# Retention scores from a head's parts stacked on 128 partitions

## The reference, cut to what matters

```
def _retention(q, k, v, gn_gain):
    q = _rope(q, pos, dk, RET_ROPE_THETA) * (dk ** -0.5)
    k = _rope(k, pos, dk, RET_ROPE_THETA)
    log_g = jnp.log(1.0 - 2.0 ** (-5.0 - jnp.arange(H, dtype=jnp.float32)))
    ...
    decay = jnp.where(diff >= 0, jnp.exp(jnp.maximum(diff, 0.0) * log_g[:, None, None]), 0.0)
    ...
    inner = jnp.einsum('bhncd,bhnkd->bhnck', qc, kc) * decay[None, :, None].astype(dt)
    o_inner = jnp.einsum('bhnck,bhnke->bhnce', inner, vc)
    ...
    mu = jnp.mean(o, axis=-1, keepdims=True)
    var = jnp.mean(jnp.square(o - mu), axis=-1, keepdims=True)
    on = (o - mu) * lax.rsqrt(var + GN_EPS) * gn_gain.astype(jnp.float32)[None, :, None, :]
```

## Time and profile before

| what | value |
|---|---|
| median of 3 runs | 2146.44 us (2146.4 to 2148.82) |
| the profiled execution's own time | 2147.04 us |
| span of its trace | 2145.2 us |
| its mean granted TensorE clock | 0.993 |
| PE busy | 98% of the span |
| DVE, ACT, POOL busy | 62%, 47%, 33% |

### The profile page before, as it was taken

One profiled execution on the slowest core, in us unless ns is written; L12 is line 12 of the kernel. 1 busy time (PEld: TensorE's weight loads), 2 busy tenths in 40 slices (PEclk: granted clock), 3 DMA queues, 4 the chain that ended last, 5 costly groups with the idle time before them and its releaser, 6 DMA issues.

```text
span 2145.2 us, 31345 instructions
## 1 busy us (share of the span) xinstructions
PE 2110.5 (98%) x10842; PEld 1784.4 (83%) x10842; DVE 1324.4 (62%) x2182; ACT 1007.1 (47%) x1771; POOL 701.9 (33%) x523
## 2 busy tenths in 40 slices
PE   8999999999999999999999999999999999999998
PEld 6878888888888888898887788888877888888886
DVE  5467774466762276775268788788768336676523
ACT  4345664543442253444234567777646325334322
POOL 2011345323233261443327701211155415133331
PEclk9999999999999999999999999999999999999998
DMA  5211235334433333443234322222264533434321
GB/s 171 79 47 67 84 112 190 101 122 153 150 124 108 98 108 113 161 138 123 94 101 156 118 69 75 79 75 79 94 202 138 185 99 118 135 132 167 104 93 65
DMA packets 73423, 248.15 MB, mean 116 GB/s; under 512 B 8080, under 2 KB 8336, under 8 KB 72944
## 3 DMA queue, kind: packets, MB, share of 16 engines
q1 hardware_dynamic: 51120, 182.08, 26.0%
q0 software_dynamic: 10496, 37.56, 5.1%
q10 hardware_dynamic: 11712, 27.27, 3.5%
HBM read 227.48 MB, written 18.87 MB: 115 GB/s over the span
## 4 chain that ended last, share of the span: by engine, by line
PE 83%; DVE 8%; ACT 2%; POOL 2%; issue 2%; DMA 1%; DVEq 0%; POOLq 0%; SPq 0%; ACTq 0%
PE bank L188 24%; PE bank L190 24%; PE bank L189 24%; PE bank L194 3%; PE bank L195 3%; POOL hid L738 2%; PE bank L2128 2%; DVE w_lo L162 1%; DMA w_raw<-stream 1%; DVE gn_r L2730 1%; PE bank L912 1%; DVE xn_lo L608 1%; ACT w_hi L157 1%; DVE h L622 1%; POOL hid L1471 1%
## 5 line engine op out<-in xcount | busy, mean ns | idle before, releaser
L162 DVE TENSOR_TENSOR w_lo<-w_raw,w_hi 128x1024 fp32r<-128x1024 f32 x337 | 454.8, 1353 | 425.1 <-ACT w_hi L157 422.2
L188 PE MATMUL bank<-xn_hi,w_hi 128*128 128x512 f32 (+1 forms) x1432 | 554.7, 387 | 4.1 <-DVE w_lo L162 2.6
L157 ACT ACTIVATE w_hi<-w_raw 128x1024 fp32r<-128x1024 f32 x337 | 354.7, 1054 | 414.0 <-PE bank L190 248.2
L189 PE MATMUL bank<-xn_lo,w_hi 128*128 128x512 f32 (+1 forms) x1432 | 539.1, 376 | 0.0
L190 PE MATMUL bank<-xn_hi,w_lo 128*128 128x512 f32 (+1 forms) x1432 | 538.8, 376 | 0.0
L188 PEld LDWEIGHTS bank<-xn_hi,w_hi 128*128 128x128 f32 x1432 | 271.1, 189 | 56.6 <-DVE h L622 5.2
L190 PEld LDWEIGHTS bank<-xn_hi,w_lo 128*128 128x128 f32 x1432 | 269.8, 188 | 50.2
L189 PEld LDWEIGHTS bank<-xn_lo,w_hi 128*128 128x128 f32 x1432 | 271.0, 189 | 45.7 <-issue 2.9
L188 PE MATMUL bank<-down_hi,w_hi 128*128 128x512 f32 x528 | 205.8, 390 | 0.0
L190 PE MATMUL bank<-down_hi,w_lo 128*128 128x512 f32 x528 | 205.4, 389 | 0.0
L189 PE MATMUL bank<-down_lo,w_hi 128*128 128x512 f32 x528 | 205.4, 389 | 0.0
(11 more groups left out here) (462 smaller groups left out, 4272.7 us busy)
## 6 DMA issues: line engine op xcount, KB each, us to landing
w_raw<-stream SPq DMA_DIRECT2D x337, 512.0 KB, 3.5
s_raw<-stream POOLq DMA_DIRECT2D x48, 512.0 KB, 6.3
spill_g<-gate_out ACTq DMA_DIRECT2D x16, 256.0 KB, 2.0
m_more<-spill_g POOLq DMA_DIRECT2D x3, 1024.0 KB, 12.5
x<-xt SPq DMA_DIRECT2D x4, 512.0 KB, 7.1
x<-xt ACTq DMA_DIRECT2D x1, 2048.0 KB, 9.3
spill_x<-x ACTq DMA_DIRECT2D x1, 2048.0 KB, 6.5
spill_ga<-ga_out ACTq DMA_DIRECT2D x8, 256.0 KB, 2.1
```

Of the source, the lines that this page charges most:

```text
L157: nc.scalar.activation(w_hi[:, slot, :], w_raw[:, slot % 2, :], ACT.Copy).then_inc(split_hi, 1)
L162: nc.vector.tensor_tensor(w_lo[:, slot, :], w_raw[:, slot % 2, :], w_hi[:, slot, :], ALU.subtract).then_inc(split_lo, 1)
L188: nc.tensor.matmul(to, a_hi, b_hi, start=start, stop=False, skip_group_check=True)
L189: nc.tensor.matmul(to, a_hi, b_lo, start=False, stop=False, skip_group_check=True)
```

## The change

`stage` and `stage_low` take the place of `high_qk` and `low_qk`, and are called for each of the eight heads. Of head h, with its rows r and the other 64 rows: ACT writes the high query to `rq_both[r]`, the high key to `rk_own[h % 2][r]` and again to `rk_mixed[other]`; POOL subtracts the low query into `rq_rest[r]`, a new tile, copies it with a DMA of its queue to `rq_both[other]` (128 KB within the on-chip memory), and subtracts the low key into `rk_mixed[r]`. The other rows of the two `rk_own` tiles are set to zero once. So `rk_own` times `rq_both` is hi*hi, and `rk_mixed` times `rq_both` is lo*hi + hi*lo: `score` issues two matmuls over 128 rows for each block in place of three over 64, eight for a head in place of twelve. It waits for the three high parts, the two low parts and the copy. `rq_both` and `rk_mixed` are single buffers, so the staging of a head waits for the scores of the head before.

Head 0 is staged within sparse attention, head 1 before iteration 0 (on ACT after the first loads of values and before highs(0), on POOL before lows(0)), and head h+2 in iteration h. In iteration 0, score(1) moves behind the second half of the fill.

```diff
--- before.py
+++ after.py
@@ -1700,6 +1700,8 @@
         rq_lo = sb("rq_lo", [P, S], F32R, A0 + 50 * K)
         rk_hi = sb("rk_hi", [P, S], F32R, A0 + 52 * K)
         rk_lo = sb("rk_lo", [P, S], F32R, A0 + 54 * K)
+        rq_both, rk_mixed, rk_own = rq_hi, rk_lo, (rk_hi, rq_lo)
+        rq_rest = sb("rq_rest", [P, S], F32R, A0 + 14 * K)
         decay = sb("decay", [P, 2, S], F32, A0 + 56 * K)
         rv_hi = sb("rv_hi", [P, 2, 2, S], F32R, A0 + 80 * K)
         rv_lo = sb("rv_lo", [P, 2, 2, S], F32R, A0 + 88 * K)
@@ -2551,6 +2553,7 @@
                                               "out", "square", "var", "root", "recip", "done", "gated", "cleared")}
             decay_in, rv_in = ([sem(f"ret_{n}_in{k}") for k in range(2)] for n in ("decay", "rv"))
             gr_in, r_low = sem("ret_gr_in"), sem("b2_r_low")
+            crossed, c_at, zeroed, z_at = sem("ret_crossed"), 0, att_sems["mask"], 3
             y = merge_sems
             y0 = merges["y"]
             fgm, fm = FIRST["b2_gm"], FIRST["b2_merge"]
@@ -2563,16 +2566,27 @@
             def score_bank(kb):
                 return (banks[0][:], banks[1][:, 0:384], banks[2][:, 0:256], banks[1][:, 384:S])[kb]
 
-            def high_qk(act, pair):
-                at_least(act, s["scored"], 8 * pair)
-                act.wait_ge(nsa["r_done"], 5 + pair)
-                nc.scalar.activation(rq_hi[:], r_qk[:, pair, :], ACT.Copy).then_inc(s["staged_hi"], 1)
-                nc.scalar.activation(rk_hi[:], r_qk[:, 4 + pair, :], ACT.Copy).then_inc(s["staged_hi"], 1)
-
-            def low_qk(pool, pair):
-                for n, (to, hi) in enumerate(((rq_lo, rq_hi), (rk_lo, rk_hi))):
-                    pool.wait_ge(s["staged_hi"], 2 * pair + n + 1)
-                    nc.gpsimd.tensor_tensor(to[:], r_qk[:, 4 * n + pair, :], hi[:], ALU.subtract).then_inc(s["staged_lo"], 1)
+            def stage(act, h):
+                at_least(act, s["scored"], 4 * h)
+                act.wait_ge(nsa["r_done"], 5 + h // 2)
+                r, other = halves(h % 2)
+                q, k = r_qk[r, h // 2, :], r_qk[r, 4 + h // 2, :]
+                nc.scalar.activation(rq_both[r, :], q, ACT.Copy).then_inc(s["staged_hi"], 1)
+                nc.scalar.activation(rk_own[h % 2][r, :], k, ACT.Copy).then_inc(s["staged_hi"], 1)
+                nc.scalar.activation(rk_mixed[other, :], k, ACT.Copy).then_inc(s["staged_hi"], 1)
+
+            def stage_low(pool, h):
+                r, other = halves(h % 2)
+                pool.wait_ge(s["staged_hi"], 3 * h + 1)
+                at_least(pool, crossed, 16 * h, c_at)
+                nc.gpsimd.tensor_tensor(rq_rest[r, :], r_qk[r, h // 2, :], rq_both[r, :], ALU.subtract
+                                        ).then_inc(s["staged_lo"], 1)
+                pool.wait_ge(s["staged_lo"], 2 * h + 1)
+                pool.dma_start(rq_both[other, :], rq_rest[r, :]).then_inc(crossed, 16)
+                pool.wait_ge(s["staged_hi"], 3 * h + 2)
+                nc.gpsimd.tensor_tensor(rk_mixed[r, :], r_qk[r, 4 + h // 2, :], rk_own[h % 2][r, :], ALU.subtract
+                                        ).then_inc(s["staged_lo"], 1)
+                pool.wait_ge(s["staged_lo"], 2 * h + 2)
 
             def decay_to(pool, h):
                 if h < 2:
@@ -2583,20 +2597,28 @@
                 pool.dma_start(decay[:, h % 2, :], decays[h]).then_inc(decay_in[h % 2], 16)
 
             def first_act(act):
-                high_qk(act, 0)
+                act.wait_ge(zeroed, z_at + 2)
+                stage(act, 0)
 
             def first_pool(pool):
-                low_qk(pool, 0)
+                for tile in rk_own:
+                    nc.gpsimd.memset(tile[:].bitcast(F32), 0.0).then_inc(zeroed, 1)
+                pool.wait_ge(zeroed, z_at + 2)
+                stage_low(pool, 0)
                 decay_to(pool, 0)
                 decay_to(pool, 1)
 
             def score(pe, h):
-                r = slice(64 * (h % 2), 64 * (h % 2) + 64)
-                pe.wait_ge(s["staged_lo"], 2 * (h // 2 + 1))
+                pe.wait_ge(s["staged_hi"], 3 * (h + 1))
+                pe.wait_ge(s["staged_lo"], 2 * (h + 1))
+                pe.wait_ge(crossed, 16 * (h + 1) + c_at)
                 for n, kb in enumerate(ORDER_K):
                     at_least(pe, s["weighted"], 4 * (h - 1) + (1, 3, 3, 4)[n])
-                    mm3(score_bank(kb), rk_hi[r, kb * P:(kb + 1) * P], rk_lo[r, kb * P:(kb + 1) * P],
-                        rq_hi[r, kb * P:S], rq_lo[r, kb * P:S]).then_inc(s["scored"], 1)
+                    w, to = slice(kb * P, (kb + 1) * P), score_bank(kb)
+                    nc.tensor.matmul(to, rk_own[h % 2][:, w], rq_both[:, kb * P:S], start=True, stop=False,
+                                     skip_group_check=True)
+                    nc.tensor.matmul(to, rk_mixed[:, w], rq_both[:, kb * P:S], start=False, stop=True,
+                                     skip_group_check=True).then_inc(s["scored"], 1)
 
             def first_pe(pe):
                 score(pe, 0)
@@ -2635,10 +2657,9 @@
                     fill(h, slot, range(0, 4))
                     if h:
                         values(h)
-                    else:
-                        score(pe, 1)
                     fill(h, slot, range(4, KT)).then_inc(used, 1)
                     if h == 0:
+                        score(pe, 1)
                         pe.wait_ge(nsa["out"], 16 + nsa_outs)
                         values(0)
                 squares_summed(HEADS - 1)
@@ -2672,6 +2693,7 @@
 
                 act.wait_ge(rv_saved, 32 * HEADS)
                 values_in(0)
+                stage(act, 1)
                 highs(0)
                 act.wait_ge(gr_saved, 16 * HEADS)
                 act.wait_ge(ga_saved, 16 * HEADS)
@@ -2681,8 +2703,8 @@
                         values_in(1)
                     elif h % 2 == 0 and h < 6:
                         values_in(h // 2 + 1)
-                    if h % 2 == 0 and h < 6:
-                        high_qk(act, h // 2 + 1)
+                    if h + 2 < HEADS:
+                        stage(act, h + 2)
                     if h + 1 < HEADS:
                         highs(h + 1)
                     ahead(high_part, act, fgm, h)
@@ -2693,7 +2715,7 @@
                     at_least(act, s["var"], h)
                     nc.scalar.activation(gn_sq[:], banks[6 + h % 2][:], ACT.Square).then_inc(s["square"], 1)
                     for k in A_TILES.get(h, ()):
-                        act.wait_ge(s["staged_lo"], 8)
+                        act.wait_ge(s["staged_lo"], 16)
                         act.wait_ge(nsa["out"], 16 + nsa_outs)
                         nc.scalar.activation(a_hi[:, k, :], a_raw[:, k, :], ACT.Copy).then_inc(y["y_hi"], 1)
                     if h == HEADS - 1:
@@ -2761,10 +2783,13 @@
                         nc.gpsimd.tensor_tensor(ws_lo[:, KOFF[kb]:KOFF[kb + 1]], weighted[:, KOFF[kb]:KOFF[kb + 1]],
                                                 ws_hi[:, KOFF[kb]:KOFF[kb + 1]], ALU.subtract).then_inc(s["lo"], 1)
 
+                pool.wait_ge(nsa["r_done"], KT)
+                stage_low(pool, 1)
                 lows(0)
                 for h in range(HEADS):
-                    if h % 2 == 0 and h < 6:
-                        low_qk(pool, h // 2 + 1)
+                    if h + 2 < HEADS:
+                        pool.wait_ge(s["lo"], 4 * (h + 1))
+                        stage_low(pool, h + 2)
                     if h + 2 < HEADS:
                         decay_to(pool, h + 2)
                     if h + 1 < HEADS:
```

## The result

The changed kernel takes 2157.54 us (median of 8 runs, 2153.43 to 2159.34); runs of the kernel before beside it give 2146.95 (8 runs, 2144.89 to 2150.14). The ratio is 1.0047, with a 95% interval of 1.0036 to 1.0058: 10.1 us slower, 7.7 to 12.5. I had forecast 2151.1 and a range up to 2157. The sign is right, the loss is twice mine.

The account below looks back on a forecast made before the run. PE's instructions and a ring of the other engines were both taken to need about 10.6 us a head; start +2.1, low clock +1.65 and collisions +0.9 made +4.7 us, forecast 2151.1 us, range 2143 to 2157.

Parts of the forecast that it names:

- the two waits for copies: At retention's start PE waits 2.8 us for score(1) and about 5 us for score(2), until the staging copies land.
- the ring: Later heads: the closed chain weigh, ws_hi, w_hi, w_lo, reciprocal, two products, weigh, without PE's matmuls, takes 10.6 us a head.
- the ring's collisions: Later heads: POOL's subtractions in the new stagings of iterations 3 and 5 lengthen DVE's L2738; +0.9 us, bounds 0 and 2.9.
- the low clock: Behind PE's waits at the start, matmuls run at the lower clock again; +1.65 us, bounds 0 and 1.65.
- the landing time L: Time from issue to landing of each of the first two staging copies; 4.5 us, between 2.5 and 6.2.
- Ring and PE: Later heads: PE would take 9.6 us against 10.6 for the other engines' chain, and wait for gn_sq by the difference.
- What PE saves: Each head's score drops the third product and takes about 1.3 us; 0.93 us saved a head, 7.4 in all.
- Place and form of the start's loss: Heads 1 and 2 are staged serially, each after the scores before; values(1) come 2.1 us later, bounds -1.9 and +5.5.
- my own steps: Start: first copy issued at 1561.1, second at 1564.5 + L, values(1) at 1569.5 + 2L, L being the copy's landing time.
- The ceiling of 2.6 us: Later heads: by the Trainium skill, each new staging could cost a whole subtraction, 2.6 us for the two iterations.
- Hidden parts: ACT's three instructions and later heads' copies cost nothing; a copy may land 4.3 us after issue without a wait.
- the heavy start: Rival: copies take 6.2 us at the start and collisions occur in every iteration; +10.1 us, 2156.5 us; chance 0.16.

Follow-up runs that it names:

- experiments 1: The kernel before with score in two 128-row matmuls per block, own staging kept, both cross products left out; 0.9994 of before.
- 7: The kernel before with ACT issuing w_hi ahead of the high parts of the next head's scores; 0.9999 of before.
- 8: The kernel before with two 128-row matmuls per block (not the reference's scores) and w_hi ahead of the next head's high parts; 0.9971 of before.
- Experiment 5: The changed kernel with a second rq_both and rk_mixed, heads 1 and 2 staged earlier, rq_rest still single; 1.0046 of before.
- Experiment 3: The changed kernel with gr_silu and the values of head pair 1 (3 MB) issued after w_hi of iteration 0; 1.0060 of before.
- experiment 13: The changed kernel with 16 and 27 filler matmuls into an unused bank ahead of score(1) and score(2); 1.0042 of before.
- experiment 2: The changed kernel with ACT copying the low query to the other 64 rows in place of POOL's DMA; 1.0027 of before.
- experiment 9: The changed kernel with two buffers by the head's parity and ACT's copy of the low query in place of the DMA; 1.0024 of before.

## Why the prediction was right and where it failed

What failed are terms of the sum: the two waits for copies, their places and the ring as the pace of the later heads are as forecast, but the +4.7 us are 9.2 in retention. Too small were the ring's collisions (+0.9, measured +2.2), the low clock (+1.65, measured 2.7), the landing time L (4.5 us, measured 5.1 and 4.9, with 0.27 and 0.19 from there to the matmul), and POOL's wait for its own semaphore before the second issue (nothing, measured 0.3). L failed in kind too, as is shown below.

**Ring and PE: right.** That the 0.93 us a head would not count is shown by experiments 1, 7 and 8 together. One refinement: with its ring relieved the kernel before keeps iterations of 10.56 us (7). PE is its bound, the ring stands right behind; the order in which I had them mattered for nothing.

**What PE saves: right.** A burst of 1.26 us, as worked out. Later iterations take 9.51 to 9.64 us wherever the ring lets them.

**Place and form of the start's loss: right; its size wrong.** Taking off the 1.94 us that came up earlier, the first copy is issued at 1561.23 (forecast 1561.1). From there, by my own steps:

- score(1) starts 5.37 us after the issue, where I had L = 4.5: 5.1 to the landing and 0.27 from there to the matmul, with the forecast issue 0.1 too early as well: +1.0 us.
- From score(1) to the second issue 4.04 us for 3.4; 0.3 of it is POOL's wait for its own subtraction, which no step of mine had: +0.64.
- Second copy 4.9 us, 0.19 more to the matmul: +0.59.
- score(2) to values(1) 7.69 us for 5.0 + 1.65: +1.04, the low clock.

These make 3.3 us, the difference of 7.06 and the forecast 2.1 + 1.65.

**The term that failed in kind is L.** I took the landing for a duration behind the issue, mid-way between rows of a loaded and an unloaded queue. Experiment 5 shows that it isn't: issued 1.9 us earlier, the copy lands at the same place. Experiment 3 shows what it hangs on: without the 3 MB the second copy takes 2.2 us, and where they go the delay goes. In six profiles the first copy lands 0.3 to 0.7 us behind rv_lo, the last load issued before it. That is no rule either. In experiment 13 rv_lo lands at 18.85, but gr_silu is issued only 0.14 us behind the copy (1.26 us in the changed kernel), and the copy lands at 22.28, after 7.4 us; in experiment 5 the second copy lands at 27.87, 2.1 us before the last of the loads issued ahead of it. Which loads a copy waits behind stays open. The numbers 5.1 and 4.9 fell inside my bounds, so as a size L was off by 0.5; as a duration it would have misled any attempt to mend the kernel by earlier stagings. For the short copies the Trainium skill ("DMA: Bandwidth & Descriptors", section "Anatomy of one DMA — SWDGE (gpsimd) path") gives a fixed cost of about 2.0 us, whatever the size; copies of 2.2 or 2.3 us in every profile with this copy agree, and none of those that PE waited for in the changed kernel was one of them.

**The clock: bound too low.** I had 1.65 us as estimate and upper end, since no row showed more. Behind waits of 3.38 and 4.14 us PE stood at the lower level, 1.2 GHz, for most of the way to values(1), 2.7 us. A bound from one row behind waits of 0.48 and 0.37 us does not bound what comes behind one ten times as long. How much of this reaches the end stays open (13).

**The ring's collisions: +2.2 for +0.9.** The interval that was 9.55 us became 10.44 (the fourth), just the 0.9 I had put there. But the second grew from 10.98 to 11.77 (its w_lo takes 3.75 us for 2.96) and the third from 11.01 to 11.48 (L2760 2.04 us for 1.59). That w_lo does not lie beside a staging: it runs beside the four ws_lo of the weighted scores, which start 0.68 us ahead of it (1.51 in the kernel before, 1.15 in experiment 2). I had put down nothing for these two: the second had its long w_lo before, and the third its staging, so I held them for full. The Trainium skill ("SBUF — State Buffer", section "Who interferes with whom") has the later of the two wait for the whole of the other operation; L2760 at 0.69 and at 2.04 us, beside a subtraction of 1.3, agrees in length (0.69 + 1.3 = 1.99), but by the recorded starts L2760 is the earlier of the two (1617.98 and 1618.16). For w_lo one operation is not enough: it got 2.25 us longer than its 1.5, and the four ws_lo take 3.35 us together. The ceiling of 2.6 us that I worked out by that page is nearer to the 2.2 by luck, since it has no w_lo in it.

Experiments 2 and 9 bear on what moved the collisions. With the same two subtractions in every staging, but without the copy that POOL issues between them (0.3 us of waiting and 0.55 for the issue), the five intervals make 53.40 and 53.41 us, 0.4 more than before: the second w_lo takes 2.22 us and the third L2761 1.59. So 1.8 of the +2.2 us go when the copy leaves POOL's order, and 0.4 stay with the subtractions of more heads, on which I had put the +0.9. That it is the 0.85 us of delay, and not something else in this edit (ACT has one more instruction), is argued from these times and not shown by itself.

**Hidden parts: right.** ACT's three instructions and the copies of heads 3 to 7 cost PE no wait in the changed kernel; the slack held though that of head 6 took 4.3 us. In experiment 13 that copy took 5.2, and PE waited 1.27 us for it. One sign came otherwise: PE waited for gn_sq in four iterations, 0.49 to 1.98 us, and not about 1 us in each.

**The sum.** 4.7 forecast; 3.3 + 1.3 are missing in retention, 9.24 in all, against 10.1 (7.7 to 12.5) measured. That is beside the first profile of the kernel before. Beside the second, which kept its clock, values(1) come 9.4 and the seventh sum of squares 11.8 us later; how often that kernel falls to the lower clock isn't known. The nearest rival was the heavy start, +10.1 and 2156.5 us. Its total is right and its make-up only in part: it has copies of 6.2 us (5.1 and 4.9 here) and no more low clock than mine. I gave it 0.16 and cut the range at 2157, half a microsecond above it, since all its terms had been taken at their ends, one of which, the clock, was no end.

## What to carry to other kernels

A small copy that PE waits for must be placed by the loads that are under way on the other queues or follow within a microsecond: ask when these drain, not how long the copy takes alone. An engine with time to spare that does the same copy is free of this, but its wait for the source then stands in its own order (2.52 us for PE in experiment 9). An instruction that is put into the order of an engine off the critical path moves all behind it, here by 0.85 us a staging, and with it what it collides with. Before a saving on the busiest engine is counted, time the closed chain of the other engines over an iteration; if it is as long, relieve it in the same edit or nothing comes out. An upper end of a range is only one if the row behind it was taken under the condition that the change will bring, here a wait of the same length ahead of it.

## What was unexpected of the hardware

- A 128 KB copy takes 2.2 us alone and 4.7 to 7.4 us beside bulk loads that another engine's queue was given before or after it (2.2 and 5.1 in the changed kernel, 6.8 and 6.4 in experiment 5, 6.8 in 3, 7.4 in 13).
- The kernel before kept the granted clock at 1.00 in one execution, with a PE wait of 0.37 us, and fell to the lower level in another, with waits of 0.48 and 0.37 us. By the seventh sum of squares the two are 2.5 us apart.
- One w_lo of 1.5 us took 2.96 us in the kernel before and 3.75 in the changed one, each beside POOL's four ws_lo (3.38 and 3.35 us together).
